# A second raw buffer for the gate panels, token turns through two banks, and copies ahead of the first tile's sigmoids

## The chip, the cores and the metric

The kernel runs on one core of a Trainium2 chip, as one launch. The metric is the device time of the whole launch in microseconds: 1438.76 us, the median of 3 runs (1438.36 to 1439.19). Less is better.

## What is computed

One hybrid decoder block on 1024 tokens with a model width of 1024, all in float32, cut from the reference:

```python
h = rmsnorm(x, norm_g)
proj = einsum('bsd,de->bse', h, w_in)        # 1024 x 10240: 8 groups of 1024, and 2048 gate logits
sb_q, sb_k, sb_v, sb_z, hg_q, hg_f, hg_i, hg_z, gate_logits = split(proj)
# stick-breaking attention, 8 heads of 128
z = q @ k.T * scale;  w = exp(log_sigmoid(z) + reverse_cumsum(log_sigmoid(-z)))   (causal)
u_sb = (w @ v * silu(sb_z)) @ w_sb_proj
# HGRN2, 8 heads of 128: gated linear recurrence, per-head rmsnorm
u_hg = (rmsnorm(hgrn2(silu(hg_q), 1 - f, log f, hg_i)) * silu(hg_z)) @ w_hg_proj
gate_sb, gate_hg = split(sigmoid(gate_logits + b_gate))
x = x + (gate_sb * u_sb + gate_hg * u_hg) @ w_out
out = rmsnorm(x, final_norm_g)
```

## The kernel before, in words

Everything is written out by hand: five instruction streams (SP for most DMAs, POOL, ACT, DVE, PE), each strictly in its own order, tied together by semaphores.

**The projection.** Panels of 128 columns of `w_in` are multiplied in pairs. A pair is a 2 x 2 block product, made with seven products (`P1, P6, P7, P5, P2, P3, P4` in this order on PE) instead of eight. Each product is 12 matmuls of 128x512: four k blocks, each as three matmuls of high and low parts (`b_hi,a_hi`, `b_hi,a_lo`, `b_lo,a_hi`, L1494), so a pair is 84 matmuls. `project(parity, n, p)` makes half a product; a pair has 14 such points `p`. There are 40 pairs: 4 for each of 8 heads (q and k; v and z; hg q and f; hg i and z), then 8 gate pairs (n = 32 to 39, called g = 0 to 7).

**Preparing a pair's weights.** SP loads both panels of a pair, 1 MB, into the one raw buffer `w_raw` (`load_pair`, L414). For each product ACT copies the raw block or a sum of blocks into `b_hi` (`split`, L681) and POOL subtracts to get `b_lo` (L567). POOL also makes the four sums t7, t5, t6, t4 (`prepare`, L610). Pair n+1 is prepared while pair n is multiplied, in the order P1, t7, P7, t5, t6, P6, P5, P2, P3, t4, P4. The load of the next pair waits for the last sum, t4 (`raw_sum`, L419). ACT does P1, P7, P6, P5, P2, P3 of the next pair at points 6, 7, 9, 10, 11, 12, and P4 at point 1 of the pair itself, followed by `copy_p1` (u3).

**Taking results.** DVE adds the products out of PSUM: u2, u3, c22, c12, c21 (`take_*`, L1093 to L1126). PE waits for some of these takes before it writes a bank again (`product_waits`, L1498).

**Heads.** `first_half(h)` multiplies pairs 0 and 1 of head h beside the HGRN2 work of head h-1; `second_half(h)` multiplies pairs 2 and 3 beside head h's stick-breaking attention: scores of tile j on PE (`scores`, L1541), two sigmoids on ACT (`sigmoids`, L760), a scan and a product on DVE (`weigh`, L1137), turns through the bank `turned`, and products with the values. `scores(h, j)` waits for the sigmoids of tile j-1 (L1547). The values and the HGRN2 inputs are turned to token order on PE by `turn_tokens` (L1534): four 128x128 transposes into the bank `attended`, then ACT copies them out, then the other four into the same bank. So the second four wait for ACT's copy of the first (L1536). `V_AT` and `I_AT` (L74, L75) say at which points this happens. Ahead of it ACT ends head h-1's norm with a logarithm and an exponential, each behind a table load (L802, L804), and the first sigmoid of head h needs a third table load (L769).

**Gate stage (L925 and L1419).** While the gate pairs are multiplied, ACT makes the gates and SP stores them to HBM (`store_gate`). Beside this the stick-breaking results `osb` (tiles e = 0 to 7, 512 KB each) and their `z` come back from HBM (`fetch_osb`, on ACT's queue), ACT makes a sigmoid, and DVE multiplies twice, rounds to `osb_hi` and subtracts to `osb_lo` (`silu_split`, L1375). Tiles 6 and 7 take the place of the operands of P1 and are fetched only in the last gate pair; their DVE work stands after the last take (L1429).

**Branch panels (L1730).** PE then multiplies eight panels of `w_sb_proj` with `osb`, eight of `w_hg_proj` with `ohg`, 48 matmuls each, in two halves on two banks. Half b of panel t+1 waits until DVE has gated half b of panel t (`gate_sb`, L1434). On DVE `gate_sb(0, 0)` stands behind the whole `silu_split` of `ohg` tile 0, which waits for `fetch_ohg(0)` on ACT's queue, and that waits for all gate stores, the last product and all `osb` steps (L978 to L992). After the panels comes the output projection (L1766).

Of the kernel before, what the change touches and what calls it, by code (L numbers as in the profile page):

```python
# [11 lines left out]
P = 128  # L12
D = 1024
# [105 lines left out]
def build(nc, x, norm_g, w_in, b_gate, lb_logits, hg_norm_g, w_sb, w_hg, w_out, final_g, out):  # L119
    ctx = ExitStack()  # L120
    with ctx:
# [23 lines left out]
        w_raw = place("w_raw", W, [2, KT, P])  # L145
        b_hi = place("b_hi", W + 8 * KB, [PRODUCTS, QUAD, P], F32R)
# [82 lines left out]
        osb_sig = tiles("osb_sig", lambda e: own_tile(e, 0))  # L229
# [9 lines left out]
        z_last = place("z_last", 2 * OPERAND, [S])  # L239
# [40 lines left out]
        w_loaded = sem("w_loaded")  # L280
        raw_sum = sem("raw_sum")
# [55 lines left out]
        osb_in = [sem("osb_in0"), sem("osb_in1"), sem("osb_in6"), sem("osb_in7")]  # L337
        ohg_in = [sem("ohg_in0"), sem("ohg_in1")]
        oz_sig = sem("oz_sig")
        oz_step = sem("oz_step")  # L340
        o_hi_ready = sem("o_hi_ready")
        osb_split = sem("osb_split")
        ohg_split = sem("ohg_split")
# [32 lines left out]
        def raw_block(rows, panel):  # L376

            return w_raw[:, panel, rows * QUAD:(rows + 1) * QUAD, :].rearrange("p k e -> p (k e)")
# [4 lines left out]
        def osb_loads(e):  # L383

            return (osb_in[e % 2], 32 * (e // 2 + 1)) if e < KT - 2 else (osb_in[e - 4], 32)
# [21 lines left out]
        def _(sp):  # L407
# [18 lines left out]
            def load_gate_pair(g):  # L426
                load_pair(N_HEAD_PAIRS + g, [GATES * D + (2 * g + i) * P for i in range(2)])
# [96 lines left out]
        def _(pool):  # L524
# [48 lines left out]
            def sum_t7(n):  # L573
                tt(part_of(b_sum, P7), raw_block(1, 1), raw_block(0, 1), ALU.subtract).then_inc(raw_sum, 1)
# [1224 lines left out]
```

## Time and profile before

| | |
|---|---|
| median of 3 runs | 1438.76 us |
| the profiled execution | 1439.45 us, its span 1437.7 us |
| mean granted TensorE clock | 0.979 |
| busy over the span | PE 94%, weight loads 78%, DVE 62%, POOL 49%, ACT 41% |
| start and first pairs | 0 to 92 us |
| heads | 92 to about 962 us, a head each 115.2 us |
| gate pairs | about 962 to 1157 us |
| gap, branch panel 0, gap | 1157 to 1179 us |
| other branch panels | 1179 to 1343 us |
| output projection | 1343 to 1438 us |

The profile is one execution. A row of a timeline gives start and duration in us, the engine, the line, the operation and its operands; in square brackets is how long the engine sat idle before it, and which work ended that. A row of the waits gives who waited for whom, with the total, the count and the longest. Matmuls overlap, so the durations of single ones are longer than their spacing. Line numbers are those of the kernel before; many DVE, ACT and POOL operations go through helpers and carry the helper's line (L1040, L653, L565), so they are told apart by their tiles.

### The profile page before, as it was taken

What the parts mean: (1) busy time and instruction counts of PE and PEld (TensorE: products, weight loads), DVE (VectorE), ACT (ScalarE), POOL (GpSimd) and SP (SyncE); (2) the same over time, 40 slices, a digit from 0 to 9 for tenths busy, and PEclk for the clock granted to TensorE, in tenths of its full rate; (3) what the DMA queues carried; (4) which work ended last, traced back from release to release, by engine and by line L of the source; (5) the groups of instructions that cost most, each with busy time, mean ns of one, the idle gap of its engine ahead of it and who ended that gap; (6) DMA issues with size and microseconds to landing.
All of it is one profiled execution on the core that took longest, in us unless ns stands there. A gap on an engine that the chain in (4) does not pass through costs nothing.

```text
span 1437.7 us, 23207 instructions
## 1 busy us (share of the span) xinstructions
PE 1350.5 (94%) x8408; PEld 1121.1 (78%) x8408; DVE 894.4 (62%) x1042; ACT 595.4 (41%) x974; POOL 708.8 (49%) x488
## 2 busy tenths in 40 slices
PE   5689999999999999999999999999998879999998
PEld 4568878888878877877887888887776768888886
DVE  4927956965974884884795696497333276545323
ACT  8326356346436535635635634643532321101131
POOL 6755744664564554564575466555556522223210
PEclk8799999999999999999999999999999999999999
DMA  5121121112211121122112111122342465433512
GB/s 147 29 74 30 60 88 30 61 31 71 76 31 59 36 84 59 31 80 69 30 61 79 39 61 30 61 83 92 103 161 102 143 238 189 154 95 117 192 43 102
DMA packets 134348, 119.41 MB, mean 83 GB/s; under 512 B 10096, under 2 KB 116592, under 8 KB 134256
## 3 DMA queue, kind: packets, MB, share of 16 engines
q1 hardware_dynamic: 125040, 92.84, 20.6%
q10 hardware_dynamic: 9216, 25.17, 5.0%
q8 instruction: 79, 1.29, 0.4%
q14 instruction: 13, 0.11, 0.0%
HBM read 88.63 MB, written 29.36 MB: 82 GB/s over the span
## 4 chain that ended last, share of the span: by engine, by line
PE 73%; DVE 8%; issue 6%; DMA 4%; POOL 4%; ACT 4%; SPq 0%; DVEq 0%; POOLq 0%; ACTq 0%
PE banks L1494 38%; PE banks L1744 11%; PE banks L1766 6%; PE banks L1572 4%; DMA w_raw<-in_w_in 4%; PE banks L1551 4%; PE banks L1562 2%; POOL b_lo L565 2%; POOL b_sum L565 2%; DVE hk L1040 1%; DVE hk L1260 1%; PE banks L1631 1%; PE banks L1606 1%; PE banks L1626 1%; PE banks L1633 1%
## 5 line engine op out<-in xcount | busy, mean ns | idle before, releaser
L1494 PE MATMUL banks<-a_hi,b_hi 128*128 128x512 f32 x1120 | 468.4, 418 | 46.3 <-POOL b_lo L565 17.8
L1494 PE MATMUL banks<-a_hi,b_lo 128*128 128x512 f32 x1120 | 445.7, 398 | 0.0
L1494 PE MATMUL banks<-a_lo,b_hi 128*128 128x512 f32 x1120 | 444.7, 397 | 0.0
L565 POOL TENSOR_TENSOR b_lo<-w_raw,b_hi 128x512 fp32r<-128x512 f32 x120 | 183.1, 1537 | 292.2 <-ACT b_hi L653 292.0
L1494 PEld LDWEIGHTS banks<-a_hi,b_hi 128*128 128x128 f32 x1120 | 215.2, 192 | 95.9 <-POOL b_lo L565 20.3
L565 POOL TENSOR_TENSOR b_lo<-b_sum,b_hi 128x512 fp32r<-128x512 f32 x120 | 172.4, 1437 | 163.7 <-ACT b_hi L653 163.6
L1494 PEld LDWEIGHTS banks<-a_hi,b_lo 128*128 128x128 f32 x1120 | 214.3, 191 | 48.3
L1494 PEld LDWEIGHTS banks<-a_lo,b_hi 128*128 128x128 f32 x1120 | 215.6, 193 | 37.5
L1142 DVE TENSOR_TENSOR_SCAN kappa<-kappa 128x128 f32<-128x128 f32 (+3 forms) x64 | 94.8, 1482 | 122.4 <-ACT kappa L770 122.4
L653 ACT ACTIVATE b_hi<-b_sum 128x512 fp32r<-128x512 f32 x120 | 75.3, 629 | 138.5 <-POOL b_sum L565 138.3
L637 POOL TENSOR_TENSOR w_lo<-w_raw,w_hi 128x1024 fp32r<-128x1024 f32 x20 | 48.2, 2414 | 152.5 <-ACT w_hi L653 152.5
L565 POOL TENSOR_TENSOR b_sum<-w_raw 128x512 f32<-128x512 f32 x80 | 116.6, 1457 | 1.5 <-PE banks L1494 1.5
L1040 DVE TENSOR_TENSOR u<-banks,u 128x512 f32<-128x512 f32 x81 | 55.6, 687 | 71.9 <-ACT u L653 67.2
L653 ACT ACTIVATE b_hi<-w_raw 128x512 fp32r<-128x512 f32 x120 | 72.9, 628 | 45.6 <-DMA w_raw<-in_w_in 45.1
L653 ACT ACTIVATE w_hi<-w_raw 128x1024 fp32r<-128x1024 f32 x20 | 21.0, 1058 | 153.1 <-DVE y_sum L1040 84.5
L653 ACT ACTIVATE wT<-banks 128x512 f32<-128x512 f32 (+2 forms) x96 | 47.5, 495 | 77.5 <-PE banks L1562 77.5
L1572 PEld LDWEIGHTS banks<-wT,v_tok 128*128 128x128 f32 x576 | 73.7, 191 | 3.7
L653 ACT ACTIVATE b_hi<-t 128x512 fp32r<-128x512 f32 x40 | 25.2, 630 | 123.0 <-POOL t L565 123.0
L1572 PE MATMUL banks<-wT,v_tok 128*128 128x128 f32 x576 | 74.5, 274 | 0.0
L1040 DVE TENSOR_TENSOR beta<-beta,kappa 128x128 f32<-128x128 f32 (+3 forms) x64 | 71.3, 1113 | 2.2
L1040 DVE TENSOR_TENSOR hk<-hk,forget 128x512 f32<-128x512 f32 x56 | 71.9, 1284 | 0.0
L565 POOL TENSOR_TENSOR b_lo<-t,b_hi 128x512 fp32r<-128x512 f32 x40 | 55.7, 1392 | 32.8 <-ACT b_hi L653 32.8
(195 smaller groups left out, 2434.9 us busy)
## 6 DMA issues: line engine op xcount, KB each, us to landing
w_raw<-in_w_in SPq DMA_DIRECT2D x80, 512.0 KB, 5.0
gate_d<-gate_out SPq DMA_DIRECT2D x16, 512.0 KB, 4.5
gate_in<-gate_d ACTq DMA_DIRECT2D x32, 256.0 KB, 3.1
x_tok<-in_x SPq DMA_DIRECT2D x8, 512.0 KB, 6.7
z_d<-z_out SPq DMA_DIRECT2D x8, 512.0 KB, 2.7
hz_d<-z_out SPq DMA_DIRECT2D x8, 512.0 KB, 2.7
osb_d<-o_sb SPq DMA_DIRECT2D x8, 512.0 KB, 5.7
ohg_d<-hq SPq DMA_DIRECT2D x8, 512.0 KB, 3.7
```

What stands on the lines that cost most here:

```text
L565: return nc.gpsimd.tensor_tensor(dst, a, b, op)
L637: nc.gpsimd.tensor_tensor(lo, w_raw[:, t % 2, :, :], hi.bitcast(F32), ALU.subtract).then_inc(panel_ready, 1)
L653: return nc.scalar.activation(dst, src, ACT.Copy)
L1040: return v.tensor_tensor(dst, a, b, op)
L1142: v.tensor_tensor_scan(back, back, back, 1.0, ALU.mult, ALU.min).then_inc(scan_done, 1)
L1260: v.scalar_tensor_tensor(out=new, in0=hk[:, (n - 1) * P:n * P], scalar=chunk_total[:, n:n + 1], in1=kv, op0=ALU.mult, op1=ALU.add).then_in ...
L1494: last = mm(bank, w[:, s, k, :], t[s][:, k, :], start=opens and k == 0 and z == 0, stop=k == QUAD - 1 and z == 2, skip_group_check=not opens)
L1551: last = mm(banks[:, 4 + c, 0:m], tile(q, j), k[:, c * m:(c + 1) * m], start=z == 0, stop=z == 2)
L1562: last = nc.tensor.transpose(tile(turned, i % 4), beta[j % 2][:, S - n + i * P:S - n + (i + 1) * P], ident[:, :])
L1572: last = mm(tile(attended, j % 4), v_tok[:, i, :], wT[:, i, :], start=i == 0, stop=i == j)
L1744: last = mm(pj[b], w[:, c, k, :], halfs(o[k], b), start=k == 0 and z == 0, stop=k == KT - 1 and z == 2)
L1766: last = mm(dst, tile(y[k], i), w[:, first:first + n, k, :], start=k == 0 and z == 0, stop=k == KT - 1 and z == 2)
```

## The change

1. **Second raw buffer.** Gate pairs alternate between `w_raw` (even g) and a new `w_other` (odd g), which lies on the blocks of `z_in0` and `gate_in`. `load_gate_pair(g)` waits for the t4 of gate pair g-2, the last user of that buffer (g = 1: for the last scores, g = 0: for the t4 of the last head pair). On SP it now stands one pair earlier in the order. The first two branch panels are loaded after gate pair 6's t4. POOL's eight gate pairs are written out instead of running in the loop.
2. **Stick-breaking tiles.** `z` of each tile is fetched to the tile's own place (`osb_z`), not to a shared one. DVE multiplies by z first, ACT then makes the sigmoid in place, DVE multiplies again, ACT (not DVE) rounds to `osb_hi`, DVE subtracts. The steps are spread over the takes of a pair. Tiles are fetched and gated by the tables `OSB_FETCHED` and `OSB_GATED`; tiles 1 and 2 share pair 3, tiles 6 and 7 are finished inside pair 7, and panel 0 is split there at point 8. `fetch_ohg(0)` no longer waits for the `osb` steps.
3. **Token turns.** All eight transposes are issued at one point (values: 1, inputs: 5), four into `attended`, four into `turned`. ACT copies both. `turn_inputs` waits for two more of DVE's reads (those of `turned`); the first `turn` of a head waits for the copies.
4. **Order on ACT.** `sigmoids(h, 0)` moves from point 0 to point 1, behind the P4 copy, `copy_p1` and both copies of the values.

```diff
-V_AT = {1: 0, 2: 1}
-I_AT = {4: 0, 5: 1}
+V_AT, I_AT = 1, 5
+OSB_FETCHED = {1: (0,), 2: (1, 2), 3: (3,), 4: (4,), 5: (5,), 7: (6, 7)}
+OSB_GATED = {2: (0,), 3: (1, 2), 4: (3,), 5: (4,), 6: (5,), 7: (6, 7)}
+        w_other = place("w_other", W + 38 * KB + 3 * BLOCK, [2, KT, P])
+        def gate_raw(g):
+            return (w_raw, w_loaded, 32 * (N_HEAD_PAIRS + 1 + g // 2)) if g % 2 == 0 else (w_other, other_loaded, 32 * (g // 2 + 1))
             def load_gate_pair(g):
-                load_pair(N_HEAD_PAIRS + g, [GATES * D + (2 * g + i) * P for i in range(2)])
+                if g == 1:
+                    sp.wait_ge(qk_done, 8 * HEADS)
+                elif g == 0:
+                    sp.wait_ge(raw_sum, 4 * N_HEAD_PAIRS)
+                else:
+                    sp.wait_ge(raw_sum, 4 * (N_HEAD_PAIRS + g - 1))
+                raw, loaded, _ = gate_raw(g)
+                for i in range(2):
+                    column = GATES * D + (2 * g + i) * P
+                    sp.dma_start(raw[:, i, :, :], by_rows(w_in[0])[:, :, column:column + P]).then_inc(loaded, 16)
...
-            for g in range(3, N_GATE_PAIRS):
-                load_gate_pair(g)
-                store_gate(g - 2, 0)
-                store_gate(g - 1, 1)
-            for t in range(2):
-                load_panel(t, w_sb[0], t * P)
-            store_gate(N_GATE_PAIRS - 2, 0)
-            store_gate(N_GATE_PAIRS - 1, 1)
+            for g in range(2, N_GATE_PAIRS):
+                if g + 2 < N_GATE_PAIRS:
+                    load_gate_pair(g + 2)
+                elif g + 2 == N_GATE_PAIRS:
+                    for t in range(2):
+                        load_panel(t, w_sb[0], t * P)
+                store_gate(g - 1, 0)
+                store_gate(g, 1)
             store_gate(N_GATE_PAIRS - 1, 0)
...
+            def take_tokens(dst, done):
+                for g, bank in enumerate((attended, turned)):
+                    act.wait_ge(tok_done, done + (g + 1))
+                    copy(dst[:, 4 * g:4 * g + 4, :].rearrange("p t e -> p (t e)"), bank).then_inc(tok_ready, 1)
...
-                    if u in V_AT:
-                        g = V_AT[u]
-                        act.wait_ge(tok_done, 4 * h + 1 + g)
-                        copy(v_tok[:, 4 * g:4 * g + 4, :].rearrange("p t e -> p (t e)"), attended).then_inc(tok_ready, 1)
+                    if u == V_AT:
+                        take_tokens(v_tok, 4 * h)
+                        sigmoids(h, 0)
-                    if u in QK_AT:
+                    if QK_AT.get(u, 0) > 0:
                         sigmoids(h, QK_AT[u])
...
+            def osb_sigmoid(e):
+                act.wait_ge(osb_times_z, e + 1)
+                nc.scalar.activation(osb_z[e][:, :], osb_z[e][:, :], ACT.Sigmoid).then_inc(osb_sig_done, 1)
+            def osb_high(e):
+                act.wait_ge(osb_gated, e + 1)
+                copy(osb_hi[e][:, :], osb_raw[e][:, :]).then_inc(osb_hi_ready, 1)
...
+                        for e in OSB_FETCHED.get(g, ()):
+                            fetch_osb(e)
+                    for order, e in enumerate(OSB_GATED.get(g, ())):
+                        if p == (7, 9)[order]:
+                            osb_sigmoid(e)
+                        if p == (11, 12)[order]:
+                            osb_high(e)
+                    if final and p == 8:
+                        split_panel(0, w_hi[:, 0, :, :])
...
-                        act.wait_ge(oz_step, 2 * (KT - 3) + 1)
+                        act.wait_ge(raw_sum, 4 * N_PAIRS)
...
-            act.wait_ge(oz_step, 2 * KT)
...
             for g in range(2, N_GATE_PAIRS):
                 n += 1
+                here = OSB_GATED[g]
                 take_u2(n, n)
+                osb_multiply(here[0])
                 take_u3(n, n)
+                for e in here[1:]:
+                    osb_multiply(e)
                 dve.wait_ge(gate_stored[1], 16 * g)
                 take_c22(GATE_PAIR, n)
-                split_osb(g - 2)
+                for e in here:
+                    osb_gate(e)
                 take_c12(GATE_PAIR, n)
+                for e in here:
+                    osb_low(e)
                 dve.wait_ge(gate_stored[0], 16 * g)
                 take_c21(GATE_PAIR, n)
-            for e in range(N_GATE_PAIRS - 2, KT):
-                split_osb(e)
...
+            def turn_tokens():
+                for bank, first in ((attended, 0), (turned, 4)):
+                    for i in range(4):
+                        last = nc.tensor.transpose(tile(bank, i), tile(turn_in, first + i), ident[:, :])
+                    last.then_inc(tok_done, 1)
```

## Rows read from the trace of the kernel before

**Rows 1.** By stretch: busy (count) of PE, PEld, DVE, ACT, POOL; PEclk, DMA, GB/s.
```profile
321.00:437.00 116.00, 113.31 (x813) 94.69 (x812) 83.45 (x100) 57.17 (x95) 64.53 (x45) 1.00 0.18 56
...
1179.00:1343.00 164.00, 164.00 (x721) 135.18 (x722) 88.81 (x103) 24.46 (x24) 40.79 (x17) 1.00 0.44 138
```

**Rows 2.** The same view for one gate pair.
```profile
1037.90:1062.10 24.20, 20.82 (x84) 16.75 (x84) 7.74 (x9) 7.74 (x12) 14.10 (x12) 0.93 0.39 130
```

**Rows 3.** PE's waits over the whole span: total us, times, longest.
```profile
PE banks L1538 <- ACT v_tok L653: 17.2, 8, 5.1
```

**Rows 4.** PE's waits from 950 to 1165 us.
```profile
PE banks L1494 <- POOL b_lo L565: 16.8, 5, 3.8
```

**Rows 5.** PE's timeline, the first of the five stalls in the gate pairs.
```profile
1041.09 0.80 PE L1494 MATMUL banks<-a_hi,b_hi 128*128 128x512 f32 x1 [3.21 <-POOL b_lo L565]
```

**Rows 6.** SP's and ACT's timelines, loads and copies of gate pairs.
```profile
1046.15 1.01 SPq L421 DMA_DIRECT2D w_raw<-in_w_in  x2
...
1026.43 0.33 ACTq L901 DMA_DIRECT2D osb_raw<-osb_d  x1
...
1030.18 0.63 ACT L653 ACTIVATE b_hi<-w_raw 128x512 fp32r<-128x512 f32 x1 [5.41 <-DMA w_raw<-in_w_in]
```

**Rows 7.** POOL's timeline, one gate pair: its P1, P6 and P4 splits.
```profile
1055.90 1.44 POOL L565 TENSOR_TENSOR b_lo<-w_raw,b_hi 128x512 fp32r<-128x512 f32 x1 [7.75 <-ACT b_hi L653]
...
1063.96 1.27 POOL L565 TENSOR_TENSOR b_lo<-t,b_hi 128x512 fp32r<-128x512 f32 x1 [0.74 <-ACT b_hi L653]
...
1071.04 1.29 POOL L565 TENSOR_TENSOR b_lo<-b_sum,b_hi 128x512 fp32r<-128x512 f32 x1 [0.74 <-ACT b_hi L653]
```

**Rows 8.** POOL's and DVE's timelines where two operations overlap.
```profile
1030.93 2.32 DVE L1040 TENSOR_TENSOR osb_lo<-osb_raw,osb_hi 128x1024 fp32r<-128x1024 f32 x1
...
1032.13 2.27 POOL L565 TENSOR_TENSOR b_sum<-w_raw 128x512 f32<-128x512 f32 x1
```

**Rows 9.** Page, costliest groups: a take on DVE, a 1024-wide copy on ACT.
```profile
L1040 DVE TENSOR_TENSOR u<-banks,u 128x512 f32<-128x512 f32 x81 | 55.6, 687 | 71.9 <-ACT u L653 67.2
...
L653 ACT ACTIVATE w_hi<-w_raw 128x1024 fp32r<-128x1024 f32 x20 | 21.0, 1058 | 153.1 <-DVE y_sum L1040 84.5
```

**Rows 10.** DMA issues, 1143 to 1158 us: KB each, us to landing.
```profile
z_last<-z_d ACTq DMA_DIRECT2D x1, 512.0 KB, 8.8
```

**Rows 11.** Page, DMA issues: the gate stores, and stores beside which little runs.
```profile
gate_d<-gate_out SPq DMA_DIRECT2D x16, 512.0 KB, 4.5
...
hz_d<-z_out SPq DMA_DIRECT2D x8, 512.0 KB, 2.7
```

**Rows 12.** Timelines of PE, ACT and DVE around branch panel 0.
```profile
1163.48 0.79 PE L1744 MATMUL banks<-osb_hi,w_hi 128*128 128x512 f32 x1 [6.16 <-POOL w_lo L637]
...
1167.01 0.33 ACTq L914 DMA_DIRECT2D ohg_raw<-ohg_d  x1
...
1172.29 2.62 DVE L1040 TENSOR_TENSOR ohg_raw<-ohg_raw,z_in 128x1024 f32<-128x1024 f32 x1 [3.40 <-DMA z_in<-hz_d]
...
1178.90 0.47 PE L1744 MATMUL banks<-osb_hi,w_hi 128*128 128x512 f32 x1 [2.45 <-DVE y_sum L1040]
```

**Rows 13.** ACT's timeline at the start of a second half (head 1).
```profile
211.07 1.28 ACT L769 ACT_TABLE_LOAD   x1
...
212.53 0.27 ACT L770 ACTIVATE kappa<-banks 128x128 f32<-128x128 f32 x1
212.69 0.63 ACT L653 ACTIVATE b_hi<-b_sum 128x512 fp32r<-128x512 f32 x1
...
213.69 0.61 ACT L653 ACTIVATE v_tok<-banks 128x512 f32<-128x512 f32 x1
```

**Rows 14.** PE's timeline: the value turns of head 0, and of head 1.
```profile
96.67 1.12 PE L1538 MATMUL banks<-ident,turn_in 128*128 128x128 f32 x4 [5.07 <-ACT v_tok L653]
...
214.35 0.66 PE L1538 MATMUL banks<-ident,turn_in 128*128 128x128 f32 x4 [1.73 <-ACT v_tok L653]
214.76 0.37 PE L1551 MATMUL banks<-k_hi,q_hi 128*128 128x256 f32 x1
```

More of the change, by code:

```diff
@@ L374, in part_of, with raw_block @@
             return b[:, s, :, :].rearrange("p k e -> p (k e)")
-        def raw_block(rows, panel):
-            return w_raw[:, panel, rows * QUAD:(rows + 1) * QUAD, :].rearrange("p k e -> p (k e)")
+        def raw_block(rows, panel, raw=w_raw):
+            return raw[:, panel, rows * QUAD:(rows + 1) * QUAD, :].rearrange("p k e -> p (k e)")
+        def gate_raw(g):
+            return (w_raw, w_loaded, 32 * (N_HEAD_PAIRS + 1 + g // 2)) if g % 2 == 0 else (w_other, other_loaded, 32 * (g // 2 + 1))
         def by_rows(w):
@@ L623, in prepare @@
                 freed(n, P2)
-                split(n, SPLIT_ORDER, P2, raw_block(1, 0))
+                split(n, SPLIT_ORDER, P2, raw_block(1, 0, raw))
                 freed(n, P3)
-                split(n, SPLIT_ORDER, P3, raw_block(1, 1))
+                split(n, SPLIT_ORDER, P3, raw_block(1, 1, raw))
                 freed(n, P4)
-                sum_t4(n)
+                sum_t4(n, raw)
                 split(n, SPLIT_ORDER, P4, part_of(b_sum, P4))
             prepare(1)
-            with pool.Fori(0, N_PAIRS - 2) as i:
+            with pool.Fori(0, N_HEAD_PAIRS - 2) as i:
                 prepare(i + 2)
+            for g in range(N_GATE_PAIRS):
+                prepare(N_HEAD_PAIRS + g, *gate_raw(g))
             def split_panel(t, hi, lo):
@@ L679, in split_first, with split @@
                 copy(part_of(b_hi, s), raw_operand(s)).then_inc(hi_ready, 1)
-            def split(n, s):
+            def split(n, s, raw=w_raw, loaded=w_loaded, count=None):
                 if made_by(s):
@@ L684, in split @@
                 else:
-                    act.wait_ge(w_loaded, 32 * n + 32)
+                    act.wait_ge(loaded, 32 * n + 32 if count is None else count)
                 act.wait_ge(product_done, products_before(n - 1, s))
-                copy(part_of(b_hi, s), raw_operand(s)).then_inc(hi_ready, 1)
+                copy(part_of(b_hi, s), raw_operand(s, raw)).then_inc(hi_ready, 1)
             norm_tiles(0, 4)
@@ L726, in copy_p1, with pair_point @@
                 copy(u3[:, :], pair_bank(pair, P1)).then_inc(p1_copied, 1)
-            def pair_point(pair, n, p, last=False):
+            def pair_point(pair, n, p, next_raw=(), last=False):
                 if p == 1:
@@ L932, in _ @@
                         finish_gate(g - 1)
-                    pair_point(n, n, p, final)
-                    if g < 2 and u in I_AT:
-                        i = I_AT[u]
-                        act.wait_ge(tok_done, 4 * (HEADS - 1) + 3 + i)
-                        copy(i_tok[:, 4 * i:4 * i + 4, :].rearrange("p t e -> p (t e)"), attended).then_inc(tok_ready, 1)
+                    pair_point(n, n, p, () if final else gate_raw(g + 1), final)
+                    if u == I_AT:
+                        take_tokens(i_tok, 4 * (HEADS - 1) + 2)
                     if g < 2 and u in HG_AT:
@@ L1532, in tile @@
                 return t[:, n * P:(n + 1) * P]
-            def turn_tokens(half, before_it):
-                need(pe, tok_ready, before_it)
-                for i in range(4):
-                    last = nc.tensor.transpose(tile(attended, i), tile(turn_in, 4 * half + i), ident[:, :])
-                last.then_inc(tok_done, 1)
+            def turn_tokens():
[3 more added lines that the diff above has]
+                    last.then_inc(tok_done, 1)
             def scores(h, j):
```

181 lines of the change are left out of this document (81 added, 100 removed).

## The prediction

> **What bounds the kernel now.** I read the stretches by engine first. In the heads PE is busy 113.3 of 116 us [rows 1], in the branch panels 164.0 of 164, both at clock 1.00: there the kernel is bound by PE, and a matmul of 128x512 comes every 164.0 / 721 = 0.2275 us (I use 0.227, a product of 12 is 2.72, a pair of 84 is 19.06). A gate pair has the same 84 matmuls but takes 24.2 us at clock 0.93 [rows 2]. PE's waits name the cause: 16.8 us in five stalls for the low parts that POOL makes, all in the gate pairs [rows 4], the first of 3.21 us at 1041.09 [rows 5]. Behind it lies a ring through the single raw buffer: the load is issued at 1046.15 when the last sum is made [rows 6], POOL's first split of it starts at 1055.90, its P6 split ends at 1065.23 (PE waits for just that), its P4 split ends at 1072.33 [rows 7]. The other wait is the one for the copy of the values, 17.2 us in eight heads [rows 3]: 5.07 in the first, 1.73 in head 1 [rows 14], some 1.7 in each of the seven. Last, PE is idle 6.16 and 2.45 us around branch panel 0 [rows 12].
>
> **Gate pairs, ideal.** Up to 1037.88 (1041.09 - 3.21, rows 5) nothing stalls PE over weights. From there to the end of the last pair, 1163.48 - 6.16 = 1157.32 [rows 12], are 119.4 us. The work is 72 + 4 x 84 = 408 matmuls, 92.6 us at full clock. All of the 26.8 us goes if nothing else is late: 16.8 are stalls [rows 4], 10.0 are matmuls at the lower clock of 1.2 GHz after them. Not every stall has that: the first matmul behind 3.21 us lasts 0.80 us [rows 5], the first behind 2.45 us only 0.47 [rows 12], and the panels after it run at clock 1.00 [rows 1]. A new stall is priced here by the row that it is nearest to, the second with no clock loss. **-26.8.**
>
> What is late next? POOL needs 1072.33 - 1055.90 = 16.4 us a pair [rows 7], less than 19.06, so POOL keeps up once it is level. It isn't level at the start, and three things eat into the gain.
>
> (a) **The first late pair, g = 3.** Its raw panels are now there 20 us early, but ACT reaches the P1 copy only behind the `osb` fetch, which waits for the last `ohg` store and is issued at 1026.43; the copy now comes at 1030.18 because of the load [rows 6]. In its place stand four DMA issues instead of two, so it comes at 1028.0 to 1030.2; POOL's P6 split ends 9.3 to 10.9 us later (9.3 from 1055.90 to 1065.23 [rows 7], 10.9 from 1030.18 to 1041.09 [rows 5, 6]). PE wants it at 1037.88. Stall between 1.0 and 3.2; I take 2.0, since the copy is nearer to 1029. **+2.0.**
>
> (b) **POOL against DVE.** A POOL operation that lies beside a DVE operation with both inputs in SBUF takes 2.27 us instead of 1.28, and DVE's 2.32 [rows 7, 8]. Today POOL idles while most of the `osb` work is done; now it works through it, three such DVE operations a tile, and two tiles in pair 3. If each costs POOL 1.0, its period is 16.4 + 3 = 19.4 with one tile and over 22 with two, so it falls behind PE by 1.4, 1.9, 0.4 and 0.4 us in pairs 4 to 7, some 4 us; if most fall into POOL's 0.74 us gaps it is nothing. I take **+1.5** (0 to 4).
>
> (c) **Tiles 6 and 7 in the last pair.** This is the new wait. DVE's order is now u2, multiply tile 6, u3, multiply tile 7, c22, and each multiply waits for a DMA. Behind it queue u3 and c22, and P3 of PE waits for c22. The fetch of both, 2 MB, is issued right behind the P4 copy, which comes 1071.04 - 0.7 - 1065.23 = 5.1 us after the P6 split if POOL is late [rows 7], or some 3 us after the start of P6 if it is level. The fourth DMA lands some 8 us after the first issue (tile 0 of `ohg`, two DMAs, takes 5.3 us [rows 12]; the last DMA of the present burst 8.8 after its own issue, beside 1 MB of panels [rows 10], which now come a pair earlier). Then 1.3 for the multiply (2.32 less the 1.0 of the collision) [rows 8] and 0.69 for c22 [rows 9]: c22 is done 3 or 5.1 + 8 + 2.0 = 13.0 to 15.1 us after P6's start, while P3 starts at 4 x 2.72 = 10.9. Stall 2.1 to 4.2, plus up to 1.5 of clock, as behind the 3.21 us [rows 5]; faster DMAs could bring it to 0. I take **+3.5** (0 to 5.6).
>
> **From the last product to branch panel 1.** Now 1178.90 - 1157.32 = 21.6 us [rows 12]. In the new order tiles 6 and 7 are done about when the product P4 is, and panel 0's split is long done, so panel 0 starts at once: the 6.16 us stall goes. But panel 1 still waits for `gate_sb(0, 0)`, behind the whole `ohg` tile 0. From P3's end: c12 0.69, gate 1.06, high copy 1.06, subtract 1.3, c21 0.69 [rows 8, 9], 4.8 in all, so c21 ends 2.1 us after P4; the gate's last half takes 0.7; the store lands 2.7 to 4.5 us later [rows 11], 3.4 with one store just ahead of it. With 0.3 for the hand-overs `fetch_ohg(0)` goes out at +6.5 instead of 1167.01 - 1157.32 = +9.7 [rows 12]. From there to PE's restart is today 1178.90 - 1167.01 = 11.9 and stays. Panel 1 starts at +18.4 instead of +21.6: **-3.2** (-4 to -1.3). PE is idle for 18.4 - 10.9 = 7.5 us in one piece, in the place of 6.16 and 2.45. Behind 6.16 us matmuls run at 1.2 GHz today (0.79 us for the first [rows 12]), and so they will behind 7.5. Today this lies within the 21.6 us (48 matmuls, 10.9 us of work, take 21.6 - 6.16 - 2.45 = 13.0 with it); then it lies behind them, in panel 1, and is paid on top: **+1.6** (0 to 2.1).
>
> **Values.** PE's wait for the copy goes, but `scores(h, 1)` waits for the sigmoids of tile 0, and these now stand behind four copies. ACT is free at 211.07 [rows 13]. Today: table load 1.28, sigmoids until 212.80, P4 copy and u3 1.00, values copy until 214.30, PE goes on at 214.35 and reaches the scores at 214.76 [rows 13, 14]. After: P4 copy and u3 1.00, two values copies 0.50 + 0.61, table load 1.28, sigmoids 0.45, that is 211.07 + 1.00 + 1.11 + 1.28 + 0.45 = 214.91, and with the same 0.05 for the hand-over the scores start at 214.96. The wait takes the other's place: +0.20 us a head, seven times **+1.4** (0 to +3.5). In head 0 the first sigmoids end today before the P4 copy, after the change behind it, and PE's 5.07 us stay within 0.5. Where ACT's table load stands among the copies makes no difference: the sum is the same.
>
> The Trainium skill (ScalarE: Activation LUTs, What ACT_TABLE_LOAD costs) prices a switch at about 1.28 us for the load and 1.38 us more for a drain, which speaks against putting the load behind copies whose pipeline must empty. By that rule seven heads would cost 7 x 1.38 = 9.7 us more. The trace agrees on the load, 1.28 us, and shows no drain around it: kappa, the second sigmoid, starts 0.18 us after the load's end [rows 13].
>
> **Inputs.** Eight transposes at point 5 instead of four at 4 and 5: the same work, no PE wait there today, and POOL's next split is as late as now. The new wait for DVE's two reads of `turned` ends before PE gets there. Nothing. The second fetch in pair 2, loads one pair earlier on SP, and the stores behind them meet no one who waits: each store's reader comes over 5 us later. Nothing.
>
> **Sum.** -26.8 + 2.0 + 1.5 + 3.5 - 3.2 + 1.6 + 1.4 = -20.0. The profiled execution took 1439.45 us, 0.69 over the median, so 1419.4 there and 1418.8 for the median; I say 1419. All bounds to the good: -26.8 + 1.0 - 4 = -29.8, 1409; I give one more. All to the bad: -26.8 + 3.2 + 4 + 5.6 - 1.3 + 2.1 + 3.5 = -9.7, 1429.
>
> **Rivals.**
> 1. *ACT and DVE in a ring.* `osb_sigmoid` and `osb_high` make ACT wait for DVE inside its own stream, `osb_low` makes DVE wait for ACT, and the next pair's copies and `finish_gate` stand behind both. For it: two tiles in pair 3. Against it: ACT and DVE are each busy 7.7 of 24.2 us [rows 2]. If it holds PE to 21.5 us a pair from pair 4 on, 4 x 2.4 = 9.6 more, less (b): -12, 1427 to 1431.
> 2. *The values' wait goes for good*, because ACT gets to the copies earlier than I read: then 1.7 x 7 = 12 us less, and 1.4 not paid: 1405. Against it: ACT has no gap from 211.07 to 214.30 [rows 13].
> 3. *Slower.* Place: the wait of `scores(h, 1)`, seven times. If it becomes as long as head 0's, 5.07 instead of 1.73 [rows 14], it is 3.3 us longer and pays for the clock besides as the stalls of the gate pairs do, another 1.8 (24.2 - 19.06 - 3.36 [rows 2, 4]): 5.1 x 7 = 36, so -21.4 + 36 = +14.6, 1453. It decides from 3.1 us a head on (21.4 / 7). Against it: every piece of ACT's chain is read [rows 13].
> 4. *The buffer does nothing*, since POOL is held by ACT's copies and not by the load. Against it: ACT's copy waits 5.41 us for the DMA [rows 6]. 1437 to 1440.
>
> **Chances.** Forecast 0.80, rival 1 0.08, rival 2 0.06, rival 3 0.04, rival 4 0.02. The range 1408 to 1429 is that of the forecast and touches rival 1. A measurement of this kernel can tell some 0.2%, 2.9 us, from no change. Faster 0.94, same 0.02, slower 0.04.
>
> **What would show it.** In the profile after: no stall over 1 us for POOL's low parts but one near 1040 us of 1 to 3 us; gate pairs of 19 to 20 us; a stall of PE before P3 of the last pair for DVE's take; panel 0 without a wait, and one stall of about 7.5 us before panel 1; in each head no wait for the values but one of about 2 us of the scores for kappa, and a head still 115.2 to 115.5 us. It is wrong if POOL's P6 split is late in every pair (then b or rival 1), if a head changes by over 0.5 us, or if panel 1 starts much earlier or later than 18 us after the last product.

## The result: 8 us less, not 20

The changed kernel takes 1430.38 us (median of 5 runs, 1429.29 to 1432.58) against 1438.36 us of the kernel before in the same comparison (5 runs, 1437.36 to 1439.19): ratio 0.9948, 95% interval 0.9933 to 0.9962. It is faster, as forecast, but by 8 us and not by 20, and 1.4 us outside the range. The profiled execution is the slowest of the five; its span is 1430.8 us against 1437.7, so the traces have 6.9 us to explain.

The stages are told apart by PE's stalls. In the gate pairs four stalls are left, three of them in these rows; the last row is the stall before panel 1. PE's timeline of after, gate stage and branch panels (start, duration, engine, line, operation, and in brackets the idle time before it and what ended it):

```profile
1048.37 0.53 PE L1517 MATMUL banks<-a_hi,b_hi 128*128 128x512 f32 x1 [2.38 <-POOL b_lo L589]
...
1078.86 0.47 PE L1517 MATMUL banks<-a_hi,b_hi 128*128 128x512 f32 x1 [0.65 <-POOL b_lo L589]
...
1144.87 0.76 PE L1517 MATMUL banks<-a_hi,b_hi 128*128 128x512 f32 x1 [4.91 <-DVE gate_out L1052]
...
1169.49 0.76 PE L1768 MATMUL banks<-osb_hi,w_hi 128*128 128x512 f32 x1 [6.59 <-DVE y_sum L1052]
```

The fourth, of 0.46 us, is at 1075.21. So where [rows 4] has 16.8 us of waits for POOL, 8.4 us are left (3.0 for POOL, 5.4 for DVE), and the 6.16 us in front of panel 0 [rows 12] are gone: it starts at once at 1151.75. The windows of the same stage (busy of PE, PEld, DVE, ACT, POOL with counts, granted clock, DMA share, GB/s):

```profile
1045.99:1067.00 21.01, 18.63 (x76) 15.24 (x76) 8.08 (x8) 9.26 (x14) 18.15 (x12) 0.92 0.43 150
1067.00:1128.00 61.00, 59.80 (x261) 48.23 (x260) 24.70 (x27) 29.11 (x44) 52.89 (x34) 1.00 0.41 138
1128.00:1152.00 24.00, 19.09 (x78) 15.06 (x77) 11.84 (x11) 12.01 (x15) 11.09 (x7) 0.93 0.35 133
```

The middle of the stage runs at clock 1.00, where one pair stood at 0.93 [rows 2]. The clock is low only behind the 2.38 and the 4.91 us. In the heads the values' wait of [rows 3] has turned into a wait of the scores:

```profile
PE banks L1574 <- ACT kappa L796: 18.2, 8, 5.7
```

That is 5.69 us in head 0 and 1.78 us in each of the seven others. The wait in the seven heads is as foretold (head 0's was to stay within 0.5 us of 5.07 and is 0.6 above it), and yet the heads have become longer:

| stretch | before | after | change | forecast |
|---|---|---|---|---|
| start and heads, to the first stall for POOL in the gate pairs | 1037.9 | 1046.0 | +8.1 | +1.4 |
| from there to the end of the last product | 119.4 | 105.8 | -13.7 | -19.8 |
| last product to panel 1 | 21.6 | 17.7 | -3.8 | -3.2 |
| panel 1 to the end | 258.8 | 261.3 | +2.5 | +1.6 |
| sum | | | -6.9 | -20.0 |

That stall begins at 1037.88 before and at 1045.99 after (1048.37 - 2.38). The 6.7 us by which the first line misses are the largest error, and the next rows show what they are: head 1 and head 2 of after, in PE's timeline, and the windows around the first matmuls of heads 1 to 4.

```profile
215.42 0.39 PE L1574 MATMUL banks<-k_hi,q_hi 128*128 128x256 f32 x1 [1.78 <-ACT kappa L796]
...
216.51 0.63 PE L1517 MATMUL banks<-a_lo,b_hi 128*128 128x512 f32 x1
216.94 0.63 PE L1517 MATMUL banks<-a_hi,b_lo 128*128 128x512 f32 x1
...
332.30 0.39 PE L1574 MATMUL banks<-k_hi,q_hi 128*128 128x256 f32 x1 [1.78 <-ACT kappa L796]
...
333.10 0.39 PE L1517 MATMUL banks<-a_lo,b_hi 128*128 128x512 f32 x1
333.33 0.39 PE L1517 MATMUL banks<-a_hi,b_lo 128*128 128x512 f32 x1
```

```profile
215.00:221.00 6.00, 5.58 (x21) 4.59 (x22) 2.52 (x5) 1.30 (x5) 0.00 (x0) 0.72 0.14 54
332.00:338.00 6.00, 5.70 (x30) 4.84 (x31) 2.96 (x6) 2.05 (x7) 0.00 (x0) 1.00 0.12 49
447.00:453.00 6.00, 5.36 (x20) 4.42 (x21) 2.52 (x5) 1.51 (x6) 0.00 (x0) 0.72 0.17 65
564.00:570.00 6.00, 5.48 (x29) 4.71 (x30) 2.74 (x6) 2.26 (x8) 0.00 (x0) 1.00 0.14 57
```

The same wait of 1.78 us is followed by matmuls every 0.43 us (1.2 GHz) in heads 1, 3, 5 and 7 and every 0.23 us (2.4 GHz) in heads 2, 4 and 6. A measure for it, used below: the time from the first to the thirteenth matmul of the projection behind the scores. It is 5.13, 5.02, 4.98 and 4.92 us in the slow heads and 3.64 in the others; before the change it is 3.65 to 3.67 in all seven, behind a wait of 1.73 us [rows 14]. The four slow heads lose 5.5 us together.

### The profile page after: what moved, and what is told of

Its sections match the earlier page's. It is cut to its first block, busy times and chain, and to the rows that moved or that the text cites. A ratio compares the mean times of both kernels' runs of the same rounds, so it can differ in the third digit from the quotient of the medians.

```text
span 1430.8 us, 23078 instructions
## 1 busy us (share of the span) xinstructions
PE 1352.5 (95%) x8408; PEld 1122.2 (78%) x8408; DVE 886.5 (62%) x1034; ACT 602.7 (42%) x982; POOL 725.8 (51%) x488
## 4 chain that ended last, share of the span: by engine, by line
PE 53%; issue 17%; POOL 15%; ACT 5%; DMA 5%; DVE 3%; SPq 0%; POOLq 0%; ACTq 0%; DVEq 0%
PE banks L1517 24%; PE banks L1768 12%; POOL b_lo L589 8%; POOL b_sum L589 7%; PE banks L1790 6%; PE banks L1598 4%; PE banks L1574 4%; DMA w_raw<-in_w_in 3%; PE banks L1588 2%; ACT b_hi L679 1%; ACT L795 1%; DVE raw_a L1052 1%; POOL t L589 1%; ACT v_tok L679 1%; ACT scT L830 1%
## 5 line engine op out<-in xcount | busy, mean ns | idle before, releaser
L589 POOL TENSOR_TENSOR b_lo<-w_raw,b_hi 128x512 fp32r<-128x512 f32 x108 | 171.4, 1597 | 265.7 <-ACT b_hi L679 265.7
L589 POOL TENSOR_TENSOR b_lo<-b_sum,b_hi 128x512 fp32r<-128x512 f32 x120 | 176.8, 1474 | 152.9 <-ACT b_hi L679 152.8
L589 POOL TENSOR_TENSOR b_sum<-w_raw 128x512 f32<-128x512 f32 x72 | 107.6, 1495 | 1.1 <-PE banks L1517 1.1
L795 ACT ACTIVATE beta<-banks 128x128 f32<-128x128 f32 (+3 forms) x64 | 41.5, 649 | 72.2 <-PE banks L1574 72.1
```

Source lines behind the costliest of these rows:

```text
L589: return nc.gpsimd.tensor_tensor(dst, a, b, op)
L795: nc.scalar.activation(keys(beta[j % 2]), score, ACT.Sigmoid, scale=SB_SCALE)
```

## Experiments

All times are medians; the kernel before took 1438.8 us in the comparisons of e1 to e8 and 1439.3 in those of e9 to e11.

### One half of the change at a time

`e1_gates_only` has the gates' buffer and tiles of the change and the heads' turns and order of the kernel before; `e2_heads_only` is the reverse. The diff is the first piece of that of e1 against the changed kernel; with it go the turns by halves and `sigmoids(h, 0)` at point 0.

```diff
-V_AT, I_AT = 1, 5
+V_AT = {1: 0, 2: 1}
+I_AT = {4: 0, 5: 1}
...
```

> The changed kernel with the token turns and the order of the first sigmoids put back as before; the second buffer, the osb steps and the end of the gate stage stay changed. In the changed kernel the heads end 8.2 us later than before, and four of the seven looped heads show 12 matmuls after the scores of tile 1 in 5.0 us instead of 3.65. Theory A (the heads' loss is made by the new wait of the scores, 0.15 us a head, and by the lower clock behind it): the heads come back to 115.2 us each, PE's first matmul after its first gate-stage stall is at about 979.9 us, total about 1438.4 - 8.0 - 7.9 = 1422.5 us. Theory B (the head loss comes with the other edits, which move code or loads): the heads stay near 116.2 us, total about 1430.

> The kernel before with only the token turns through two banks and the first sigmoids behind the copies. Theory A: the heads lose 8 us, total about 1446, and heads with a low clock behind an unchanged wait of 1.8 us appear again, some with and some without. Theory B, and the step of the prediction (0.2 us a head, no clock loss): about 1440.

Measured: e1 1424.95 us (1424.56 to 1428.21), ratio 0.9914 [0.9897, 0.9930]; e2 1445.01 us (1444.23 to 1446.82), ratio 1.0044 [1.0027, 1.0061]. So the gates' half gives 13.8 us and the heads' half costs 6.3. In e1 the heads are back at 115.2 us on average, and the measure at 3.64 or 3.65. In e2 the measure reads 5.23, 3.64, 5.09, 3.64, 5.02, 3.64, 4.89 in heads 1 to 7, with 1.78 us of wait in each. The loss in the heads belongs to the head's pieces alone and has nothing to do with the new buffer.

### Where the first sigmoids stand on ACT

`e3_sig_first` keeps the turns through two banks and puts the first sigmoids back at point 0; `e4_sig_between` puts them between the two copies of the values. The diff is e3's.

```diff
                     if u == V_AT:
                         take_tokens(v_tok, 4 * h)
-                        sigmoids(h, 0)
...
-                    if QK_AT.get(u, 0) > 0:
+                    if u in QK_AT:
                         sigmoids(h, QK_AT[u])
```

> The changed kernel with one edit: the sigmoids of tile 0 stand again at point 0, ahead of the P4 copy, the two copies of the values behind them. The scores of tile 1 then find kappa ready (212.8 us against PE's 213.4), and the copies end near 214.9, before the first turn needs them (about 215.7). If the wait is only a matter of ACT's order, PE waits for neither: each of seven heads takes 115.2 - 1.7 = 113.5 us, head 0 about 2 us less, total 1430.4 - 7 x 2.8 - 2 = 1409 us. Rival: the first turn now waits for the copies, 1 to 2 us a head, and the total stays within 3 us of 1430.

> The changed kernel with the first sigmoids between the two copies of the values: PE's wait of the scores for kappa is 0.5 us shorter, 1.3 instead of 1.8. Theory A1 (behind this wait the clock falls because of its length): no head with 5.0 us for 12 matmuls, heads of 114.8 to 114.9 us, total about 1430.4 - 7 x 0.5 - 4 x 1.5 = 1421. Theory A2 (whether the clock falls is a matter of when the wait comes, not of 0.5 us more or less): some heads still lose 1.4 us, total 1425 to 1428.

e3 takes 1411.43 us (1409.84 to 1413.68), ratio 0.9813 [0.9797, 0.9830], 19.0 us less than the changed kernel. From e1 it differs by the turns through two banks alone, and takes 13.5 us less than e1: that is what the second bank is worth. In heads 1 to 7 PE has neither wait; a head takes 113.7 us; only head 0 still waits 3.8 us for the values. ACT's timeline of e3 in head 1 shows why both can go:

```profile
207.68 1.28 ACT L795 ACT_TABLE_LOAD   x1
...
209.14 0.27 ACT L796 ACTIVATE kappa<-banks 128x128 f32<-128x128 f32 x1
209.30 0.63 ACT L679 ACTIVATE b_hi<-b_sum 128x512 fp32r<-128x512 f32 x1
...
210.30 1.10 ACT L679 ACTIVATE v_tok<-banks 128x512 f32<-128x512 f32 x2
```

PE goes from its projection to the scores at 209.50 without a gap, 0.1 us after kappa is there, and nobody waits for `v_tok` at 211.4: with two banks the second transposes no longer need the first copy. In the changed kernel the same ACT work stands in the other order:

```profile
212.53 1.07 ACT L679 ACTIVATE v_tok<-banks 128x512 f32<-128x512 f32 x2
213.62 1.28 ACT L795 ACT_TABLE_LOAD   x1
...
215.09 0.27 ACT L796 ACTIVATE kappa<-banks 128x128 f32<-128x128 f32 x1
```

The two-bank turn takes the wait away, and the fourth part of the change puts one of the same length in front of the scores. Here too no drain is seen around the table load: it starts 0.02 us behind the copies' end, and the first sigmoid, at 214.92, 0.02 us behind the load. The Trainium skill (ScalarE: Activation LUTs, What ACT_TABLE_LOAD costs) prices such a drain at 1.38 us; these rows bear out only its 1.28 us for the load.

e4 takes 1422.06 us (1420.63 to 1423.53), ratio 0.9883 [0.9866, 0.9899]. PE's timeline, head 1:

```profile
212.81 0.39 PE L1577 MATMUL banks<-k_hi,q_hi 128*128 128x256 f32 x1 [1.30 <-ACT kappa L796]
```

The wait for kappa is 1.30 us, and the measure is 3.64 to 3.67 in all seven heads: 0.48 us less of wait gives the whole clock back, heads of 114.9 us.

### The length of the wait

`e9_long_after` and `e10_long_before` lengthen the wait by writing one copy of the values in 16 pieces: in e9 the second of the changed kernel, in e10 the first of the kernel before. The diff is e10's.

```diff
-                        copy(v_tok[:, 4 * g:4 * g + 4, :].rearrange("p t e -> p (t e)"), attended).then_inc(tok_ready, 1)
+                        parts = 16 if g == 0 else 1
+                        whole, w = v_tok[:, 4 * g:4 * g + 4, :].rearrange("p t e -> p (t e)"), 512 // parts
+                        for i in range(parts):
+                            last = copy(whole[:, i * w:(i + 1) * w], attended[:, i * w:(i + 1) * w])
+                        last.then_inc(tok_ready, 1)
```

> The changed kernel; ACT copies the second half of the values in 16 pieces of 32 columns in place of one of 512, so that the first sigmoids come later and PE's wait of the scores for kappa grows from 1.78 us by 0.4 to 2.0 us a head. Theory L (behind a short wait it is its length that decides whether PE falls to the lower clock; 1.78 lies on the edge, 1.30 below it): all seven heads lose the 1.3 to 1.5 us behind it, not four, so three more heads lose 4 us, plus seven times the added wait: 1437 to 1450, and the 12 matmuls behind the scores take 4.9 us or more in each of heads 1 to 7. Rival (what counts lies outside the wait, in the phase of the clock against the heads): some heads stay at 3.64 us.

> The kernel before; ACT copies the first half of the values in 16 pieces of 32 columns in place of one of 512, so that PE's stall between the two sets of transposes grows from 1.73 us by 0.4 to 2.0 us. Theory L (length alone): from about 1.8 us on this wait loses clock as well, in part or all of the seven heads, 12 matmuls behind the scores 4.9 us or more there: 1438.8 + 7 x (0.4 to 2.0) + 4 x 1.4 and more, 1447 to 1463. Rival (place: a wait between transposes loses no clock, one in front of the scores does): all seven heads stay at 3.66 us, and the kernel is slower only by the seven added waits, 1441.6 to 1453.

e9 takes 1442.08 us (1438.34 to 1447.58), ratio 1.0025 [1.0009, 1.0040]; e10 1450.73 us (1445.37 to 1457.13), ratio 1.0077 [1.0044, 1.0110]. The second time lies in the ranges of both of its theories, so the matmuls decide. PE's timeline, heads 1 and 2 of e9 and then head 2 of e10:

```profile
217.11 0.58 PE L1578 MATMUL banks<-k_hi,q_hi 128*128 128x256 f32 x1 [2.71 <-ACT kappa L800]
...
334.78 0.39 PE L1578 MATMUL banks<-k_hi,q_hi 128*128 128x256 f32 x1 [2.72 <-ACT kappa L800]
```

```profile
333.28 0.66 PE L1542 MATMUL banks<-ident,turn_in 128*128 128x128 f32 x4 [2.68 <-ACT v_tok L653]
```

| kernel | wait of PE in heads 1 to 7 | first to thirteenth matmul, heads 1 to 7 |
|---|---|---|
| e4 | 1.30, scores | 3.64 to 3.67 in all |
| before, e1 | 1.73, between turns | 3.64 to 3.67 in all |
| after | 1.78, scores | 5.13, 3.64, 5.02, 3.64, 4.98, 3.64, 4.92 |
| e2 | 1.78, scores | 5.23, 3.64, 5.09, 3.64, 5.02, 3.64, 4.89 |
| e5 (below) | 1.78, scores | 5.22, 3.64, 5.04, 3.64, 5.00, 3.64, 4.95 |
| e6 (below) | 1.79, scores | 5.00, 3.66, 3.66, 5.23, 3.66, 5.05, 3.66 |
| e11 (below) | 1.78, scores | 3.65, 3.64, 3.65, 5.23, 3.65, 5.23, 3.65 |
| e10 | 2.68, between turns | 4.20, 5.23, 4.36, 3.65, 5.24, 4.36, 5.23 |
| e9 | 2.72, scores | 4.56, 5.23, 4.57, 5.22, 4.56, 5.22, 6.07 |

The values of 4.20 to 4.57 are slow heads as well: there the lower clock begins earlier, in the scores or the transposes (0.58 us for the first score matmul of e9's head 1, 0.39 in head 2), so part of the loss lies outside the measure.

A place between transposes doesn't protect: that wait loses the clock too once it is 2.68 us long. Whether 1.73 us is spared for its length or for its place no run shows, since neither kernel has 1.78 us between transposes. The length matters, but not as an edge of its own. After, e5, e6 and e11 are the same program up to the gate stage, and at 1.78 us they lose the clock in four, four, three and two of seven heads, and not in the same ones; at 2.68 us one head is still spared. The first stall of the gate pairs, at the same point of e1 and e9, says the same (PE's timeline, the first matmul and the thirteenth):

```profile
1040.47 0.52 PE L1523 MATMUL banks<-a_hi,b_hi 128*128 128x512 f32 x1 [2.27 <-POOL b_lo L590]
...
1044.91 0.40 PE L1523 MATMUL banks<-a_hi,b_hi 128*128 128x512 f32 x1
```

```profile
1061.32 0.50 PE L1521 MATMUL banks<-a_hi,b_hi 128*128 128x512 f32 x1 [2.27 <-POOL b_lo L589]
...
1064.17 0.39 PE L1521 MATMUL banks<-a_hi,b_hi 128*128 128x512 f32 x1
```

Twelve matmuls take 4.44 us in the one and 2.85 in the other. Even a stall of 3.37 us in e10's gate pairs, at 1056.51, is followed by 2.87. The expectation that all seven heads lose held for e9 in the count of heads (three of them stay under its 4.9 us) and failed for head 4 of e10. That count is of one execution: e9's profiled one took 1446.69 us, 4.6 over the median, and no trace shows how many heads were slow in the shorter ones. What makes the choice in a given head isn't settled. The rows say only that it is no property of the code of that head.

### The stall in the last pair and the end

`e5_c22_first`: in the last pair, where `final` is true, DVE takes u2, u3 and c22 before it multiplies tiles 6 and 7.

```diff
                 take_u2(n, n)
-                osb_multiply(here[0])
+                if not final:
+                    osb_multiply(here[0])
                 take_u3(n, n)
-                for e in here[1:]:
-                    osb_multiply(e)
+                if not final:
+                    for e in here[1:]:
+                        osb_multiply(e)
                 dve.wait_ge(gate_stored[1], 16 * g)
                 take_c22(GATE_PAIR, n)
+                if final:
+                    for e in here:
+                        osb_multiply(e)
```

> The changed kernel; in the last gate pair DVE takes u2, u3 and c22 before it multiplies tiles 6 and 7. Theory C (the 4.91 us stall before P3 of the last pair is the wait of DVE's queue for the fetched tiles, and costs its length plus the slow matmuls behind it): the stall is gone, the gate pairs end 4.9 to 6.5 us earlier. But the osb steps of tiles 6 and 7 now come behind c22, so c12, the last high and low parts and c21 come later against the last product by 2 to 4 us, and with them the last gate store, the fetch of ohg tile 0 and panel 1. In sum 1427 us, between 1425 and 1429. Rival (the stall is something else's, the takes or the gate store): the stall stays within 1 us and the time stays at 1430.

1429.68 us (1429.15 to 1430.55), ratio 0.9941 [0.9925, 0.9956]: expected was 1427, and nearly nothing came. The mechanism was right: the 4.91 us are gone and the last product ends at 1145.5, 6.3 us earlier. But PE's timeline of e5 in front of panel 1 reads

```profile
1152.45 0.51 PE L1774 MATMUL banks<-osb_hi,w_hi 128*128 128x512 f32 x1 [1.12 <-DVE osb_lo L1052]
1168.41 0.76 PE L1774 MATMUL banks<-osb_hi,w_hi 128*128 128x512 f32 x1 [9.46 <-DVE y_sum L1052]
```

Panel 1 starts at 1168.41 instead of 1169.49. Its start hangs on c21, the last gate store and the fetch of `ohg` behind it (issued at 1156.90, in after at 1157.83), and c21 stands on DVE behind the same tiles in either order. The stall of 4.91 us had cover: the chain of the last gates was as long beside it.

`e6_ohg_early` cuts that chain: the fetch of `ohg` tile 0 and of its gate goes out in the last pair at point 8, and panel 1's copy and tile 0's sigmoid follow panel 0's.

```diff
                     if final and p == 8:
                         split_panel(0, w_hi[:, 0, :, :])
+                        act.wait_ge(w_ready, PRODUCTS * N_PAIRS)
+                        act.wait_ge(product_done, done + P6 + 1)
+                        fetch_ohg(0)
+                        act.wait_ge(raw_sum, 4 * N_PAIRS)
+                        act.wait_ge(gate_stored[0], 16)
+                        for b in range(2):
+                            act.dma_start(gate_in[:, b, :], halfs(gate_d[0], b)).then_inc(gate_loaded[b], 16)
             finish_gate(N_GATE_PAIRS - 1)
+            act.wait_ge(product_done, PRODUCTS * N_PAIRS)
+            split_panel(1, w_hi[:, 1, :, :])
+            gate_ohg(0)
...
-            act.wait_ge(product_done, PRODUCTS * N_PAIRS)
-            fetch_ohg(0)
-            fetch_gate(0)
...
```

> The changed kernel; the fetch of ohg tile 0 and of its gate is issued in the last gate pair at point 8, behind the last preparation, and not after the last product and the last gate store; panel 1's copy and tile 0's sigmoid follow right behind panel 0's. Theory D (the 6.59 us of PE before panel 1 and the slow clock behind it are the chain from c21 over the last store to this fetch): PE's wait for y_sum before panel 1 falls to under 1 us, and the panels behind it run at full clock: 1421.5 us, between 1420 and 1424. Rival (DVE itself is late there, with the low parts, c21 and silu_split of tile 0 one behind the other): at least 3 us of the wait stay, 1425 to 1428.

1423.03 us (1421.83 to 1424.69), ratio 0.9893 [0.9878, 0.9908]. The wait for `y_sum` is gone altogether, and the panels behind it keep full clock: they take 258.6 us to the end, in after 261.3. Of the 7.9 us between the two profiled spans 1.9 arise ahead of the gate pairs and are not the edit's: three heads lose the clock in place of four, and head 0 is reached 0.7 us earlier. And the last stall grew from 4.91 to 7.44 us, which the expectation did not have; e11 shows what that is.

### POOL beside DVE

`e11_small_two` leaves DVE almost nothing to do in two of its three operations on tiles 0 to 5; the gating of these tiles is left out. A first form, `e7_small_osb`, narrowed the subtraction as well. It left columns of `osb_lo` unwritten that PE reads, and there is no time of it.

```diff
-                tt(osb_raw[e][:, :], osb_raw[e][:, :], osb_z[e][:, :], ALU.mult).then_inc(osb_times_z, 1)
+                tt(osb_raw[e][:, 0:(S if e >= 6 else 8)], osb_raw[e][:, 0:(S if e >= 6 else 8)], osb_z[e][:, 0:(S if e >= 6 else 8)], ALU.mult).then_inc(osb_times_z, 1)
...
```

> The changed kernel, but DVE's two multiplications of each stick-breaking tile 0 to 5 take 8 columns in place of 1024 (these tiles' gating is not computed); the subtraction and tiles 6 and 7 are whole. Theory B (POOL is late in the gate pairs because its operations stretch beside DVE's wide ones): POOL's stretched operations fall from three to at most one a tile, the stalls of 0.46 and 0.65 us in pairs 3 and 4 are gone or halved, the last fetch is issued 3 to 4.5 us after the start of P6 in place of 5.8, and the last stall falls from 4.9 to 2 to 4 us: 1426 to 1429. Rival (the overlap costs nothing on PE's path): the fetch, the 4.9 us stall and 1429.5 to 1431 stay.

1423.26 us (1420.94 to 1424.61), ratio 0.9888 [0.9867, 0.9909]: less than either theory had. Part of it is none of its doing: two slow heads in place of four, and with them the first stall of the gate pairs begins 3.7 us earlier (1043.60 - 1.30 against 1045.99). POOL's groups from 1046 to 1137 us (line, operation, count, busy, mean ns), after and then e11:

```profile
L589 POOL TENSOR_TENSOR b_sum<-w_raw 128x512 f32<-128x512 f32 x4 | 8.1, 2030 | 0.0
```

```profile
L589 POOL TENSOR_TENSOR b_sum<-w_raw 128x512 f32<-128x512 f32 x4 | 5.2, 1292 | 0.0
```

So the stretching is real and costs 0.74 us in each of these. On PE the stalls of pairs 3 and 4 fall from 0.46 and 0.65 to 0.21 and 0, and the first from 2.38 to 1.30, 2.0 us in all. Twelve matmuls behind the first take 2.87 us in place of 4.46, and from the first stall to the last it is 4.8 us less in sum. Not all of that is shown to be POOL's: the 0.46 us is a wait for DVE, which has less to do here, and whether the clock falls behind a stall of this size is in part chance. The fetch of tiles 6 and 7 goes out 2.9 us after the start of P6 instead of 5.8. Still the last stall is 4.61 us, where 2 to 4 were expected. DVE's and POOL's timelines of e11 there:

```profile
1131.98 3.33 DVE L1052 TENSOR_TENSOR osb_raw<-osb_raw,osb_z 128x1024 f32<-128x1024 f32 x1 [1.67 <-DMA osb_z<-z_d]
...
1131.89 2.34 POOL L663 TENSOR_TENSOR w_lo<-w_raw,w_hi 128x1024 fp32r<-128x1024 f32 x1 [6.50 <-ACT w_hi L679]
```

and those of after:

```profile
1142.89 1.23 DVE L1052 TENSOR_TENSOR osb_raw<-osb_raw,osb_z 128x1024 f32<-128x1024 f32 x1 [1.17 <-DMA osb_z<-z_d]
...
1143.31 3.04 POOL L663 TENSOR_TENSOR w_lo<-w_raw,w_hi 128x1024 fp32r<-128x1024 f32 x1 [6.51 <-ACT w_hi L679]
```

Whoever starts first keeps its own length, and the other ends late. Tile 7 landed 0.09 us after panel 0's subtraction had begun on POOL, and the multiply for which c22 and PE wait took 3.33 us instead of 1.23. In after, e1 and e3 tile 7 came first and the stall is 4.6 to 4.9 us; in e4 and e6 it came second (3.40 and 3.20 us) and the stall is 7.4; that of e11 is no longer than 4.61 because its fetch went out 2.9 us earlier. This is a new collision made by putting panel 0's split inside the last pair. The Trainium skill (SBUF — State Buffer, SBUF: two separate sides) says that the port pair which the two engines share is an exclusive lock for a whole instruction; these rows agree to within 0.2 us (1131.89 + 2.34 + 1.23 = 1135.46; the multiply ended at 1135.31).

### All three together

`e8_all_three` has the edits of e3, e5 and e6.

> The changed kernel with three edits together: the first tile's sigmoids back at point 0 (alone 1411.4), the last pair's takes ahead of tiles 6 and 7, and the early fetch of ohg tile 0. If each gain stands by itself: 1411.4 - 5.5 - 9 = 1397, since the late end chain that the second edit makes is then no longer on the path; between 1395 and 1402. If the third edit's gain goes to a wait for DVE instead: 1402 to 1407.

1401.84 us (1399.34 to 1403.36), ratio 0.9751 [0.9737, 0.9764]: 28.5 us faster than the changed kernel, and at the upper end of what was expected. Alone e3 gave 19.0 us, e6 7.4 and e5 0.7, some 27 in sum, so the gains add up. That c22 first is worth more now that the end chain is short is likely but not shown: no run has e3 and e6 without it. Of the early fetch's gain 2.1 us go to a wait for DVE before panel 1. Its largest waits from 930 us on:

```profile
PE banks L1530 <- DVE gate_out L1059: 3.9, 4, 1.6
PE banks L1530 <- POOL b_lo L589: 2.9, 2, 2.2
PE banks L1781 <- DVE y_sum L1059: 2.1, 1, 2.1
```

## What the forecast had right, and the step that failed

The step that failed is the same in three terms: the forecast priced a new wait by its length alone and gave nothing for the slow matmuls behind it. In the heads' term, +1.4 forecast and +8.1 measured, that is 5.5 us; in (a) and (c) it is 3.2.

**The gate pairs.** Right in mechanism: POOL keeps up, the ring through the single buffer is gone, and what is late next is what was named, in the named places. The waits were sized well: (a) 2.38 us against 2.0; (b) 0.46 + 0.65 = 1.1 in stalls against 1.5, though PE waits for POOL only in the 0.65, in the 0.46 for DVE; (c) 4.91 against 3.5, inside its bounds, with the fetch 5.8 us after P6's start where 5.1 was the later of two cases. Together 8.4 against 7.0. In the prediction it is the sentence that prices a new stall by the nearer of two rows and with no loss of clock. It said this of the 2.45 us in [rows 12]; but behind 2.38 us nine matmuls stand 0.42 us apart (+1.8), and behind 4.91 us seven (+1.4). For (a) chance had a part: behind a stall of 2.21 us (e4) and one of 2.27 us (e9) at the same place nothing was lost. For (c) that loss was written into the bound and left out of the value. The other 1.5 us are gaps of 0.3 to 0.5 us between matmuls behind the short waits and at the borders of pairs, which had no term. 1.4 + 3.2 + 1.5 = 6.1, the gap between -19.8 and -13.7.

**The last product to panel 1.** Right: panel 0 starts at once, `fetch_ohg(0)` is issued 6.1 us after the last product (forecast 6.5), panel 1 starts at +17.7 (18.4). The idle piece is 6.59 us long, the clock behind it falls, and twelve matmuls at 0.43 us cost 2.5 us where 1.6 with an upper bound of 2.1 was given. e5 shows that (c) and this term were not independent: priced alone, each looks like a gain for whoever removes it, but the chain of the second covers most of the first.

**The heads.** This is the term that was mis-sized most: +8.1 against +1.4. The arithmetic of ACT's chain was right: the wait changed its place and grew by 0.05, and from head 1's scores to head 7's it is 696.56 us against 691.45; less 4.2 of clock in heads 1, 3 and 5 that is 0.15 a head, where 0.20 was forecast: seven times 0.15 is 1.0. Once more the missing price is the clock, 5.5 us in four heads. The other 1.6 of the 8.1 are 0.6 at head 0, 0.8 just ahead of the second gate pair (967 to 980 us before), and 0.2 of small gaps. The 0.8 come with the gates' half, for e1 has them too; the rows show a new wait among them,

```profile
974.94 0.50 PE L1603 MATMUL banks<-quad_hi,mean_w 128*128 128x512 f32 x1 [0.40 <-DVE scT L1052]
```

which the kernel before and e2 don't have; why DVE is late there is open. Rival 3 had the right mechanism (the scores' wait with a loss of clock behind it) but was tied to the wait growing to 5 us. It needed no such growth: 1.78 us in front of the scores is enough part of the time. Either 1.73 us was already that near, or its place between the transposes spared it; no run tells these two apart. The forecast read the 3.21 us row as slow and the 2.45 and 1.73 us rows as fast and put a border between them; but the row of 2.45 us was a single one, and behind 1.78 us some heads are slow and some are not.

**The inputs and the DMAs moved** were put at nothing. For the inputs no row shows a cost. For the loads and fetches that moved it isn't shown: the new wait of 0.40 us above belongs to the gates' half, of which they are a part.

**The range.** Its lower end was worked out with all bounds to the good; its upper end, 1429, had no clock loss for (a), (b) and the heads. With 5.5 and 1.8 added it would have reached 1436.

## What to carry to other kernels

In this kernel, price each PE stall of 1.8 us or more with the slow matmuls behind it, mostly 1.3 to 1.8 us where it happens and 2.5 behind 6.59 us, and with both ends where rows disagree; a stall that is merely moved can then cost what it didn't before. When two edits take a wait away together, ask what each does alone: here the second bank removed the wait and the new order on ACT put one back, 19 us in sum. A profile is one execution: a count of slow heads in it is a sample. And before a stall is counted as a gain, look for the chain beside it that ends at the same place.

## What the runs showed of the hardware that wasn't expected

- Identical heads with an identical wait of 1.78 us are followed by 1.2 GHz in some heads and by 2.4 GHz in others, alternating in after, e2 and e5, otherwise placed in e6 and e11. At 1.30 us the fall never happened in 7 heads, at 1.73 us never in 14, at 2.68 us in 6 of 7, at 2.72 us in 7 of 7, each counted in one execution. At one and the same place, behind 2.27 us, it happened in e1 and not in e9.
- A DVE multiply of 128x1024 with both inputs in SBUF takes 1.23 us alone and 3.2 to 3.4 us if a POOL subtraction of that size (2.34 us alone) began just before it. A tile that landed 0.42 us ahead of that subtraction (after) had a stall of PE of 4.91 us behind it, one that landed 0.02 us behind its start (e4) one of 7.40.
